# Six small constant transfers move from SyncE's queue to ScalarE's, and a smaller DMA scratch: a two-layer diffusion trunk on one core

## The reference

```
mod_x = (silu(c) @ w_ada[l] + b_ada[l])          # also for c_ctx
h = rmsnorm(s, g) * (1 + m[3*i+1]) + m[3*i]
s = s + 0.5 * m[3*i+2] * ((silu(h @ wg) * (h @ wu)) @ wd)
lam = exp(sum(lq1*lk1)) - exp(sum(lq2*lk2)) + lam_init
```

## Time and profile before

| | |
|---|---|
| time, median of 3 runs | 2836.54 us (2836.24, 2836.54, 2841.76) |
| the profiled execution's own time | 2838.13 us |
| span, from its first to its last instruction | 2836.2 us |
| mean granted TensorE clock | 0.983 |
| TensorE busy (matmul) | 2715.3 us, 96% |
| DVE, ACT, POOL busy | 1687.2, 763.9, 197.8 us |
| DMA, all on one queue | 253.90 MB, 27.8% of the 16 engines |
| chain that ended last | PE 89%, DVE 5%, ACT 2%, POOL 2%, SP's queue 1% |

### The profile page before, as it was taken

How to read it: one execution, slowest core, us unless ns; L and a number is a source line. 1 busy time by engine, 2 the same in 40 slices (tenths; PEclk the granted TensorE clock), 3 DMA queues, 4 the chain that set the end, 5 groups by cost and what they waited for, 6 DMA issues and landing times.

```text
span 2836.2 us, 38296 instructions
## 1 busy us (share of the span) xinstructions
PE 2715.3 (96%) x15352; PEld 2307.2 (81%) x15352; DVE 1687.2 (59%) x2403; ACT 763.9 (27%) x1131; POOL 197.8 (7%) x324
## 2 busy tenths in 40 slices
PE   6999999999987999999999999999999988899998
PEld 4888888888955878888888788888887956888887
DVE  5655655668837375656556756556348845544445
ACT  4211212133147232111121412111124155322222
POOL 2000000030003210000001200000002013100001
PEclk7999999999999999999999999999999999999999
DMA  7532333321111132333322233323122111132221
GB/s 269 177 121 89 104 104 92 97 79 60 45 47 43 45 104 90 116 106 98 109 89 89 81 98 104 104 93 128 45 70 65 60 60 39 54 116 89 89 89 45
DMA packets 180757, 255.35 MB, mean 90 GB/s; under 512 B 5311, under 2 KB 128813, under 8 KB 180653
## 3 DMA queue, kind: packets, MB, share of 16 engines
q1 hardware_dynamic: 180652, 253.90, 27.8%
HBM read 251.78 MB, written 2.10 MB: 90 GB/s over the span
## 4 chain that ended last, share of the span: by engine, by line
PE 89%; DVE 5%; ACT 2%; POOL 2%; SPq 1%; issue 1%; DMA 0%; DVEq 0%; POOLq 0%; ACTq 0%
PE ps L931 27%; PE ps L932 27%; PE ps L933 27%; PE ps L1322 1%; PE ps L1346 1%; PE ps L1267 1%; POOL sqsum L922 1%; DVE nb L2142 1%; DVE h_lo L1785 1%; PE ps L1334 1%; ACT e L1639 1%; PE ps L1072 1%; ACT w_hi L1419 1%; DVE rstd L1764 1%; POOL w_lo L834 0%
## 5 line engine op out<-in xcount | busy, mean ns | idle before, releaser
L931 PE MATMUL ps<-h_hi,w_hi 128*128 128x512 f32 (+1 forms) x3040 | 1048.9, 345 | 18.7 <-DVE h_lo L1785 17.5
L933 PE MATMUL ps<-h_hi,w_lo 128*128 128x512 f32 (+1 forms) x3040 | 1042.6, 343 | 0.0
L932 PE MATMUL ps<-h_lo,w_hi 128*128 128x512 f32 (+1 forms) x2928 | 1007.1, 344 | 0.0
L931 PEld LDWEIGHTS ps<-h_hi,w_hi 128*128 128x128 f32 x3040 | 582.2, 192 | 91.6 <-issue 19.4
L933 PEld LDWEIGHTS ps<-h_hi,w_lo 128*128 128x128 f32 x3040 | 581.6, 191 | 66.1
L932 PEld LDWEIGHTS ps<-h_lo,w_hi 128*128 128x128 f32 x2928 | 561.2, 192 | 64.7 <-issue 1.5
L1884 DVE TENSOR_TENSOR prod<-sil,ps 128x512 f32<-128x512 f32 (+1 forms) x156 | 87.9, 568 | 640.3 <-PE ps L933 633.3
L931 PE MATMUL ps<-hid_hi,w_hi 128*128 128x512 f32 (+1 forms) x1248 | 432.9, 347 | 0.0
L932 PE MATMUL ps<-hid_lo,w_hi 128*128 128x512 f32 (+1 forms) x1248 | 429.2, 344 | 0.0
L933 PE MATMUL ps<-hid_hi,w_lo 128*128 128x512 f32 (+1 forms) x1248 | 429.0, 344 | 0.0
L1419 ACT ACTIVATE w_hi<-raw 128x2048 fp32r<-128x2048 f32 x158 | 297.1, 1907 | 470.9 <-PE ps L933 470.9
(11 more groups left out here) (157 smaller groups left out, 1970.2 us busy)
## 6 DMA issues: line engine op xcount, KB each, us to landing
side_raw<-in_w_ada SPq DMA_DIRECT2D x120, 512.0 KB, 3.7
raw<-in_w_ffn_gate SPq DMA_DIRECT2D x44, 1024.0 KB, 5.3
raw<-in_w_ffn_up SPq DMA_DIRECT2D x44, 1024.0 KB, 5.3
raw<-in_w_ffn_down SPq DMA_DIRECT2D x44, 1024.0 KB, 4.9
raw<-in_w_in SPq DMA_DIRECT2D x14, 1024.0 KB, 5.3
ada_buf<-in_w_ada SPq DMA_DIRECT2D x9, 1024.0 KB, 10.5
raw<-in_w_out SPq DMA_DIRECT2D x8, 1024.0 KB, 5.1
raw<-in_w_in SPq DMA_DIRECT2D x8, 512.0 KB, 5.2
```

What stands on the lines that cost most here:

```text
L931: mm(out, wh, xh, start=start, stop=False)
L932: mm(out, wh, xl, start=False, stop=False)
L933: return mm(out, wl, xh, start=False, stop=stop)
```

## The change

Six `dma_start` calls leave SP's program. They stand now at the head of ACT's, ahead of `take_vector(3)`, in the order vecc, sel, vec0, vec1, lams, vecw, with the same sources, destinations and semaphores. What SP keeps has the order it had. Besides, the program is built with 1024 bytes of scratch for dynamic transfers in each partition in place of 16384, so that all tiles start 15360 bytes lower.

```
@@ SP's program
             for t in (4, 5):
                 load_tokens(t, ctx_landed)
-            for src, dst in ((a["vecc"], vstage[0:3 * KD, 2, :]), (a["sel"], sel[:])):
-                sp.dma_start(dst, src).then_inc(cond_landed, 16)
             for t in range(4):
                 load_tokens(t, x_landed)
...
             for b in BEFORE[:3]:
                 for half in range(2):
                     load_ada(b, half)
-                if b == 0:
-                    for src, dst in ((a["vec0"], vstage[0:NROW, 0, :]), (a["vec1"], vstage[0:NROW, 1, :]),
-                                     (a["lams"].broadcast_to((128, DEPTH * 4 * HD)), lamv[:]...)):
-                        sp.dma_start(dst, src).then_inc(const_landed, 16)
-                    sp.dma_start(tapstage[:], a["vecw"]).then_inc(taps_landed, 16)
@@ ACT's program
+            for src, dst in ((a["vecc"], vstage[0:3 * KD, 2, :]), (a["sel"], sel[:])):
+                act.dma_start(dst, src).then_inc(cond_landed, 16)
+            for src, dst in ((a["vec0"], vstage[0:NROW, 0, :]), (a["vec1"], vstage[0:NROW, 1, :]),
+                             (a["lams"].broadcast_to((128, DEPTH * 4 * HD)), lamv[:]...)):
+                act.dma_start(dst, src).then_inc(const_landed, 16)
+            act.dma_start(tapstage[:], a["vecw"]).then_inc(taps_landed, 16)
             take_vector(3, ccol[:].rearrange("p i k -> p (i k)"))
@@ kernel()
-    nc = bacc.Bacc("TRN2", target_bir_lowering=False, num_devices=1)
+    nc = bacc.Bacc("TRN2", target_bir_lowering=False, num_devices=1, dynamic_dma_scratch_size=1024)
```

More of the change, by code:

```diff
@@ L711, in _ @@
                     load_ada(b, half)
-                if b == 0:
-                    for src, dst in ((a["vec0"], vstage[0:NROW, 0, :]), (a["vec1"], vstage[0:NROW, 1, :]),
-                                     (a["lams"].broadcast_to((128, DEPTH * 4 * HD)), lamv[:].rearrange("p l i n -> p (l i n)"))):
-                        sp.dma_start(dst, src).then_inc(const_landed, 16)
-                    sp.dma_start(tapstage[:], a["vecw"]).then_inc(taps_landed, 16)
             def release(key):
@@ L1697, in take_vector @@
                 act_fn(dst, ps[:, bank_of(("vec", i)), 0:VECTORS[i][0]], ACT.Copy).then_inc(bank_free[bank_of(("vec", i))], 1)
+            for src, dst in ((a["vecc"], vstage[0:3 * KD, 2, :]), (a["sel"], sel[:])):
+                act.dma_start(dst, src).then_inc(cond_landed, 16)
+            for src, dst in ((a["vec0"], vstage[0:NROW, 0, :]), (a["vec1"], vstage[0:NROW, 1, :]),
+                             (a["lams"].broadcast_to((128, DEPTH * 4 * HD)), lamv[:].rearrange("p l i n -> p (l i n)"))):
+                act.dma_start(dst, src).then_inc(const_landed, 16)
+            act.dma_start(tapstage[:], a["vecw"]).then_inc(taps_landed, 16)
             take_vector(3, ccol[:].rearrange("p i k -> p (i k)"))
```

## The result

| | before | after |
|---|---|---|
| median | 2838.01 us (20 runs) | 2841.86 us (20 runs) |
| profiled execution, span | 2838.13, 2836.2 us | 2841.06, 2839.3 us |
| first activation of ACT | 10.08 us | 17.99 us |
| block 3 landed | 43.36 us | 41.2 us |
| shift and scale | 49.18 us | 52.44 us |

The change makes the kernel 3.9 us slower by the medians: ratio 1.0016, interval 1.0010 to 1.0023. The time lies within the predicted range of 2832.5 to 2844.0 and within the 0.2% called no change. But the interval is clear of 1, the size is well above the +0.7 us forecast, and 2841.86 lies above the narrower band of 2835.0 to 2839.5 in which the forecast itself put it.

A forecast was written before the change was run, and what follows sets the result against it. TensorE bounds the kernel from 76 us; before that block 3's landing sets the start. Landing 0, ACT 0 to +1.5, constants 0 and scratch 0 gave +0.7 us, a median of 2837.2 us, range 2832.5 to 2844.0.

The forecast's parts named there:

- Part 1, the landing: Start, SP without the small transfers: block 3 still lands at about 43.36 us, change 0, between 3.7 earlier and 1 later.
- The bound of 3.7 us: Start, block 3's landing: at most 3.7 us earlier, if the small rows slip in between the large pieces for free.
- the second sign named: Start, changed profile: block 3 lands within 1.5 us of 43.36, and one DMA engine lags by microseconds towards the end.
- The first sign named: Start, changed profile: no SP issue longer than 2 us before block 2, DMA shares near 1 from 16 to 22 us.
- Part 2, ACT: Head of ACT: lams' issue held until 17.4 us, cover to 15.9, path of 33.3 us behind; costs 0 to +1.5 us.
- The turns: ACT's and SP's queues on one DMA engine: one piece of each alternately, 0.196 us a pair with tokens, 0.110 with 2 KB pieces.
- Part 3, the constants: Start, DVE and TensorE waiting for vectors and lams: later arrival costs nothing, with 4.7 and 2.5 us of cover.
- Part 4, the scratch: Whole kernel, tiles 15360 bytes lower: no effect, 0, between -0.5 and +0.5 us.
- The sum: Whole kernel: landing 0, ACT 0 to +1.5, constants 0, scratch 0, together +0.7 us; median 2837.2 us.
- ACT is held long: Rival, ACT's queue: fewer small rows fit or fewer turns, ACT free at 24.6, path 8.7 us late, 2845.2 us; chance 0.22.
- The gain comes through: Rival, start: small rows cost large ones nothing, ACT's queue goes first, block 3 lands 3.7 us earlier, 2832.8 us; chance 0.22.
- The fifth sign: After 76 us, changed profile: every distance is as before; a difference would make the reasoning, not just a term, wrong.

The follow-up runs named there:

- e2_act_wait18: The kernel before, nothing moved, with ACT waiting at its head until the second half of modulation block 0 has landed; 2843.42 against 2837.89 us, ratio 1.0021.
- e7_wait13: The kernel before, nothing moved, with ACT waiting at its head until the latent tokens have landed; 2836.36 against 2837.34 us, ratio 1.0001.
- e5_warm: The kernel after with 40 extra matmuls on constants ahead of the turn of block 0; 2841.47 against 2837.34 us for before, ratio 1.0015.
- e1_order: The kernel after with lams and vecw ahead of vec0 and vec1 on ACT's queue; 2837.68 against 2837.89 us for before, ratio 1.0001.
- e3_scratch: The kernel before with only the dynamic scratch set to 1024 bytes, no transfer moved; 2837.42 against 2837.89 us, ratio 1.0000.
- e8_move: The kernel after with the six transfers moved but the scratch left at 16384 bytes; 2840.94 against 2837.34 us for before, ratio 1.0018.
- e6_pad_act: The kernel after with vec0 and vec1 padded from 107 to 128 rows; 2833.60 against 2837.34 us for before, ratio 0.9985.
- e4_pad_sp: The kernel before with vec0 and vec1 padded from 107 to 128 rows, still on SP's queue; 2834.59 against 2837.89 us, ratio 0.9992.
- e12_warm22_again: The kernel after with 22 extra matmuls ahead of the turn of block 0, run a second time; 2841.97 against 2838.05 us for before, ratio 1.0011.
- e10_four_on_act: The kernel after with lams and vecw back on SP's queue behind block 0; 2835.22 against 2837.23 us for before, ratio 0.9993.

## Why the prediction held, and where its sizes were off

**Part 1, the landing.** Forecast no movement, measured 2.1 us earlier. The step that failed is "the engine that has vec0 and vec1 has exactly the same work before block 3 as it had". The lagging tail after 44 us is there, as this step wants it, but what lags then was issued behind block 3. Nor do the small rows fall behind it: ACT's queue moves nothing after 28 us, and DVE had lams by 27.38, long before block 3. So either that engine did have some 2 us of idle time in the kernel before, or a small row costs it less than 23 ns when it takes turns with large pieces. No run tells these apart, and it stays open. The bound of 3.7 us was right to the tenth, and it takes rows spread over all engines to reach it. By the second sign named, a landing within 1.5 us of 43.36, this part failed. The first sign named, no SP issue over 2 us before block 2, was put too strictly: the six halves stood 15.20 us at a full queue, which costs nothing while the share is 1.05.

**Part 2, ACT.** This is the step that decides, and it was right in kind: the issue of lams stands behind the 214 rows, ACT was free at 16.69 (forecast 17.4), POOL's additions stay 15.64 us long, 2.75 behind the first activation. Two terms were missing, which made +1.5 into +3.3 us at shift and scale. The table load had hidden in the idle time before 10.08; behind the issues it is on the path, 1.28 us, so the first activation is at 17.99. And the path is 34.45 us long, not 33.3: I had let the root follow ACT's table load, but it waits 0.93 us and the second reciprocal 0.24 more for the statistics' matmuls. These stand on TensorE behind the turn of block 1, and at half clock they take 2.91 us instead of the 1.54 of before. So 0.6 for the start, 1.2 for the length. `e2_act_wait18` and `e7_wait13` show both the price and the cover, and `e5_warm` shows the part of the clock.

How I reached 17.4 is less well founded than the hit suggests, and part of it was luck. The turns are there, but faster than the 5.1 and 9.1 rows a microsecond of the sum (6 and 9.8), and by the count above 48 vec rows had gone by 6 us. Against that, more rows had to go: the issue of lams ended with 96 rows left and 118 gone, not with 130 left and 95 pieces gone, 10 of them of vecc and sel. The two misses nearly cancel; at the forecast's own turns 118 rows would have made T about 21 us (an estimate from its terms). Nor is the rule a depth alone. In `e1_order` vec1's issue ended when, by the same count, 89 rows of vec0 were still ahead of it, which is near the 96, but in the kernel after the same issue went through at once with all 107 ahead. When an issue is held by another is open. The Trainium skill ("DMA: Bandwidth & Descriptors", section "Issuing engines are not separate DMA queues") says that spreading saves time at issue only; here it moved that time, from 12.2 us on SP to 13.1 us on ACT.

**Part 3, the constants.** Covered, as forecast. lams was in use at 27.38 (the last row was forecast for 29.7), and the dots end at 32.5, almost 12 us before the reciprocals. Their first row:

```profile
27.38 0.62 DVE L2228 TENSOR_TENSOR lamp<-lamv 128x64 f32<-128x64 f32 x1 [7.76 <-DMA lamv<-in_lams]
```

**Part 4, the scratch.** Nothing beyond 0.1%, shown by `e3_scratch`; `e8_move` loses as much without it.

**The sum.** Of the two ends of part 2, 0 and +1.5, half was taken. The trace says 3.26 us at shift and scale, 3.1 in the span. The medians differ by 3.9. The rest is no more than single executions gain or lose in the later stages (the distances below), but where the medians get it isn't shown.

**The rivals.** "ACT is held long" is the mechanism that occurred: with 96 rows left instead of 130 the queue did hold fewer small rows, but ACT was free at 16.7 and not at 24.6. "The gain comes through" failed twice: the landing moved by 2.1 us and not 3.7, and the late ACT ate that too. In `e6_pad_act`, with the rows spread, the landing moves by 3.7 us and the time by 3.7 us; that the two are the same number is chance, since ACT's path sets the end there.

**Distances after 76 us.** They are not quite fixed. The fifth sign took that for granted and said that a difference would make the reasoning wrong; it was put too strictly, since executions differ there whatever the start does. The same reciprocal in the last two stages of layer two, in the kernel after and in `e4_pad_sp`:

```profile
2143.12 1.75 DVE L1763 RECIPROCAL rstd<-std 128x256 f32<-128x256 f32 x1 [2.51 <-ACT std L1429]
2435.13 1.75 DVE L1763 RECIPROCAL rstd<-std 128x256 f32<-128x256 f32 x1 [2.27 <-ACT std L1429]
```

```profile
2134.43 1.75 DVE L1764 RECIPROCAL rstd<-std 128x256 f32<-128x256 f32 x1 [2.51 <-ACT std L1436]
2428.92 1.75 DVE L1764 RECIPROCAL rstd<-std 128x256 f32<-128x256 f32 x1 [2.27 <-ACT std L1436]
```

After, it is 292.0 us from the one to the other (291.4 before); in `e4_pad_sp` 294.5. That kernel was 6.6 us ahead of before at the first and 3.5 at the second, so 3.1 us of its gain went here. From 2284 to 2434 its granted clock was 0.94, against 0.98 in the corresponding 2291 to 2441 of before. So in this execution 5.4 us at first tn became 3.5 at the end. `e2_act_wait18` has the same long distance, 294.5: its profile was 2.8 us behind before at first tn, 1.3 at the first mark and 4.4 at the second, so what it lost beyond the start it lost here. `e12_warm22_again` has 294.0, and the profiles of the other eleven kernels have 291.4 to 292.0. What decides between the two isn't shown.

## What to carry to other kernels

Before a small transfer goes to another engine's queue, read two things: on how many DMA engines its rows run (a share of 0.07 in a full queue is one), and what the issuing engine has queued behind the issue, up to the moment that sets the end. Compare that engine's start plus its whole path, table load included, with what sets the end now; beyond that an issue that stands shows in the time. Cure the shape of the transfer first: 107 rows padded to 128 cut SP's wait at the two transfers from 8.9 to 4.2 us and removed ACT's, and gave 3.3 us by the medians without any move; the move on top of it has no gain shown.

## What the runs showed of the hardware

- Two issues of 107 rows of 512 B on an otherwise nearly empty queue let the next issue on that engine stand for 13.12 us; with 128 rows it took 0.51 us. The padded rows are more bytes and less time.
- Which issue stands depends on the order, and not on the number of pieces alone: the one behind the two vec transfers in the kernel after (13.12 us), vec1 in `e1_order` (8.8 us), none in `e10_four_on_act` (0.87 us for both vec issues).
- Two queues share one DMA engine: rows of 512 B on one went at 6 a microsecond beside pieces of 4 KB on the other, and at 9.8 beside pieces of 2 KB, in the kernel after.
- A start made 3.7 and 3.4 us shorter by keeping the granted clock at 1.00 was there in two of two profiled executions and absent from both medians, of 11 and 10. A gain of this size in the start isn't won until the timed runs show it.
- One stage of the same work, 2141 to 2432 us in the kernel before, took 291.4 to 292.0 us in eleven profiles and 294.0 to 294.5 in three; in `e4_pad_sp`, one of the three, the granted clock was 0.94 where before had 0.98.
